# A Hymba-style block with a two-level MLP: the weight loads of the MLP move from SyncE's queue to GpSimd's

## What is computed

```python
h = rms_norm(x, attn_norm)                       # x: 1024 tokens x 1024
proj = h @ w_in                                  # 1024 x 3352
y = concat(rms_norm(nsa_mixer(...)), hgrn2_mixer(...))
x = x + y @ w_out
h = rms_norm(x, mlp_norm)
x = x + square(relu(h @ w_mlp_in)) @ w_mlp_out   # 1024 -> 4096 -> 1024
```

## Time and profile before

| | before |
|---|---|
| median of 3 runs | 1528.97 us (1526.45 to 1530.16) |
| the profiled execution's own time | 1530.4 us |
| its span, first to last instruction | 1528.6 us |
| PE busy | 1442.6 us, 94% of the span |
| DVE, ACT, POOL busy | 876.9, 629.2, 162.5 us |
| granted clock of PE, mean | 0.978 of full speed |
| loads of w_mlp_in | 32, 512 KB each, median 4.8 us from issue to landing |
| loads of w_mlp_out | 64, 256 KB each, median 5.2 us |
| loads of hidden pieces | 112, 256 KB each, median 2.7 us |
| DMAs issued by POOL | none |

### The profile page before, as it was taken

The page is one execution under the profiler, slowest core; times in us unless marked ns, Lnnn a source line. Parts: engine busy times, 40 slices in busy tenths (PEclk is TensorE's granted clock), DMA queues, the critical chain, the costliest instruction groups (busy, mean ns, idle before and its releaser), DMA issues.

```text
span 1528.6 us, 23025 instructions
## 1 busy us (share of the span) xinstructions
PE 1442.6 (94%) x7958; PEld 1233.3 (81%) x7958; DVE 876.9 (57%) x1633; ACT 629.2 (41%) x1242; POOL 162.5 (11%) x179
## 2 busy tenths in 40 slices
PE   6999999999989898998989969999999699999999
PEld 6888888878878788888978857888888588888887
DVE  2002682016666565769783485666666369668764
ACT  5014212134545444460340355755555354444441
POOL 2433333520000000000122000000000000000000
PEclk9999999999999899999999989999999899999999
DMA  4211123200000000012011013444444484843342
GB/s 163 63 48 49 48 68 91 62 7 1 2 1 0 1 0 1 0 42 111 29 42 42 29 35 127 153 146 153 153 154 148 172 303 125 275 145 97 97 118 83
DMA packets 78249, 129.25 MB, mean 85 GB/s; under 512 B 8974, under 2 KB 26827, under 8 KB 78155
## 3 DMA queue, kind: packets, MB, share of 16 engines
q1 hardware_dynamic: 77968, 128.01, 26.1%
q10 hardware_dynamic: 186, 0.08, 0.0%
HBM read 94.51 MB, written 33.55 MB: 84 GB/s over the span
## 4 chain that ended last, share of the span: by engine, by line
PE 85%; DVE 8%; issue 3%; ACT 3%; DMA 1%; DVEq 0%; SPq 0%; ACTq 0%
PE ps L516 60%; PE ps L2093 7%; PE ps L2053 4%; PE ps L2068 4%; PE ps L2116 3%; PE ps L2087 1%; PE ps L1922 1%; DVE hgrn_vg L1630 1%; PE ps L755 1%; PE ps L2058 1%; PE ps L1894 1%; PE ps L2037 1%; DVE hgrn_A L1596 0%; DVE hgrn_k L1587 0%; DVE x1T_t_low L1655 0%
## 5 line engine op out<-in xcount | busy, mean ns | idle before, releaser
L516 PE MATMUL ps<-mlp_w_high,hidden_high 128*128 128x512 f32 x448 | 174.3, 389 | 0.0
L516 PE MATMUL ps<-mlp_w_low,hidden_high 128*128 128x512 f32 x448 | 174.3, 389 | 0.0
L516 PE MATMUL ps<-mlp_w_high,hidden_low 128*128 128x512 f32 x448 | 174.3, 389 | 0.0
L516 PE MATMUL ps<-w_high,hT_high 128*128 128x512 f32 (+1 forms) x448 | 170.8, 381 | 1.6 <-DVE hT_low L1351 0.9
L516 PE MATMUL ps<-w_high,hT_low 128*128 128x512 f32 (+1 forms) x448 | 168.2, 375 | 0.0
L516 PE MATMUL ps<-w_low,hT_high 128*128 128x512 f32 (+1 forms) x448 | 168.1, 375 | 0.0
L2093 PE MATMUL ps<-nsa,probs_T 128*128 x1056 | 138.6, 276 | 0.0
L1288 ACT ACTIVATE mlp_w_high<-mlp_w_raw 128x512 fp32r<-128x512 f32 x112 | 70.8, 632 | 151.6 <-PE ps L516 143.3
L1661 DVE TENSOR_TENSOR mlp_w_low<-mlp_w_raw,mlp_w_high 128x512 fp32r<-128x512 f32 x112 | 77.1, 691 | 96.0 <-ACT mlp_w_high L1193 96.0
L2093 PEld LDWEIGHTS ps<-nsa,probs_T 128*128 128x128 f32 x1056 | 130.1, 194 | 0.0
L1741 DVE TENSOR_TENSOR mlp_w_low<-mlp_w_raw,mlp_w_high 128x512 fp32r<-128x512 f32 x112 | 77.4, 691 | 68.1 <-ACT mlp_w_high L1288 68.1
(11 more groups left out here) (232 smaller groups left out, 2936.9 us busy)
## 6 DMA issues: line engine op xcount, KB each, us to landing
hidden_raw<-hidden_pieces SPq DMA_DIRECT2D x112, 256.0 KB, 2.7
mlp_w_raw<-in_w_mlp_in_dram SPq DMA_DIRECT2D x32, 512.0 KB, 4.8
hidden_pieces<-hidden SPq DMA_DIRECT2D x64, 256.0 KB, 2.3
mlp_w_raw<-in_w_mlp_out_dram SPq DMA_DIRECT2D x64, 256.0 KB, 5.2
w_raw<-in_w_in_dram SPq DMA_DIRECT2D x56, 256.0 KB, 2.7
hidden_pieces<-hidden_s SPq DMA_DIRECT2D x48, 256.0 KB, 2.2
x_in<-in_x_dram SPq DMA_DIRECT2D x8, 512.0 KB, 6.9
w_raw<-in_w_out_dram SPq DMA_DIRECT2D x16, 256.0 KB, 2.6
```

The lines of the kernel that those rows point to most:

```text
L516: ins = nc.tensor.matmul(out_ap, a_hl[i], b_hl[j], start=first and n == 0, stop=last and n == 2, skip_group_check=onto_a_sum_already_read)
```

## The change

GpSimd issues all loads of `w_mlp_in` and `w_mlp_out`; SP keeps the stores and loads of the hidden pieces and the output. The bytes, the destinations and the semaphores that the loads raise stay the same. POOL's part comes behind its last `split_to`. The waits are these:

- `load_w1(0)` and `load_w1(1)`: as before. `load_w1(p)` for p from 2: the same count of `w1_low`, no longer behind the store of h00.
- W2 (1,1), first round: wait for product a(15), no longer between the first eight `load_h`. W2 (0,0): for b(15). W2 (0,1) and (1,0): for the end of the first product.
- second round: the same counts of `w2_lows`, no longer between `load_h`.
- SP's wait for b(15) ahead of the first `load_h` is gone; its wait for `w1_low` stays.

```diff
@@ SP @@
-            sp.wait_ge(w_used, W_OUT_AT + 8)
-            load_w1(0)
-            sp.wait_ge(xt_low, 8)
-            load_w1(1)
...
             for p in range(NPAIR):
                 sp.wait_ge(h00_ready, p + 1)
                 store(1, p, h00[p % 2][:], h00_sent[p % 2])
-                if p + 2 < NPAIR:
-                    sp.wait_ge(w1_low, IN_AT["g", p] + 1)
-                    load_w1(p + 2)
...
-            sp.wait_ge(in_done, IN_AT["b", NPAIR - 1] + 1)
             sp.wait_ge(w1_low, NPROD)
             for c in range(NCPS):
                 load_h(c)
-                load_w2((1, 1), 0, c)
             store_after_e_and_f(NPAIR - 1)
-            for c in range(NCPS):
-                load_w2((0, 0), 0, c)
             store_after_g(NPAIR - 1)
...
@@ POOL, behind its last split @@
+            def load_w1(p):
+                for j in range(2):
+                    pool.dma_start(w1_raw[:, p % 2, j, :, :], w_mlp_in[0, j * BW:(j + 1) * BW, 2 * p * P:2 * (p + 1) * P]
+                                 .rearrange("(k p) c -> p k c", p=P)).then_inc(w1_loaded[p % 2][j], 16)
+
+            pool.wait_ge(w_used, W_OUT_AT + 8)
+            load_w1(0)
+            pool.wait_ge(xt_low, 8)
+            load_w1(1)
+
+            for p in range(2, NPAIR):
+                pool.wait_ge(w1_low, IN_AT["g", p - 2] + 1)
+                load_w1(p)
...
+            pool.wait_ge(in_done, IN_AT["a", NPAIR - 1] + 1)
+            for c in range(NCPS):
+                load_w2((1, 1), 0, c)
+            pool.wait_ge(in_done, IN_AT["b", NPAIR - 1] + 1)
+            for c in range(NCPS):
+                load_w2((0, 0), 0, c)
+            pool.wait_ge(in_done, NPROD)
+            for c in range(NCPS):
+                load_w2((0, 1), 0, c)
+            for c in range(NCPS):
+                load_w2((1, 0), 0, c)
+            for first, parts in ((4, ((1, 1), (0, 0))), (5, ((0, 1),)), (6, ((1, 0),))):
+                for c in range(NCPS):
+                    pool.wait_ge(w2_lows, first * NCPS + c + 1)
+                    for q in parts:
+                        load_w2(q, 1, c)
```

More of the change, by code:

```diff
@@ L874, in _ @@
                     store_after_e_and_f(p)
[L876 to L879, removed]
             def load_h(k):
@@ L891, in _ @@
                 load_h(c)
-                load_w2((1, 1), 0, c)
             store_after_e_and_f(NPAIR - 1)
-            for c in range(NCPS):
-                load_w2((0, 0), 0, c)
             store_after_g(NPAIR - 1)
[L897 to L903, removed]
-                load_h(k)
[L905 to L917, removed]
+            for k in range(W2_RING, NPROD):
+                load_h(k)
             for g, blocks_ in ((N_OUT - 5, ((0, 0),)), (N_OUT - 2, ((1, 1), (0, 1))), (N_OUT - 1, ((1, 0),))):
@@ L978, in _, with load_w2 @@
                          m % 4, W_OUT_AT + m - m % 4 - 8 if m >= 8 else None)
+            def load_w1(p):
[9 more added lines that the diff above has]
+                load_w1(p)
+            def load_w2(q, s, c):
+                p = NCPS * s + c
+                pool.dma_start(w2_raw[q][:, c, :], w_mlp_out[0, (2 * p + q[0]) * P:(2 * p + q[0] + 1) * P, q[1] * BW:(q[1] + 1) * BW])\
+                    .then_inc(w2_loaded[q, c // 2], 16)
+            pool.wait_ge(in_done, IN_AT["a", NPAIR - 1] + 1)
[14 more added lines that the diff above has]
+                        load_w2(q, 1, c)
         @block.scalar
```

## The result

| | before | after |
|---|---|---|
| median of the runs on one chip (4 each), us | 1529.57 | 1550.28 |
| lowest to highest | 1526.45 to 1531.51 | 1547.55 to 1552.53 |
| span of the profiled execution | 1528.6 | 1545.5 |
| granted clock over the span | 0.978 | 0.977 |

The ratio is 1.0121 (95% interval 1.0099 to 1.0143): slower by 18.5 us of 1529.57 (the two medians of the table differ by 20.7), forecast +5.5. The sign was right, the size was not: it is more than three times the forecast one. The forecast started from a median of 1528.97; with the ratio that gives 1547.5 us, near the top of the stated range of 1523.5 to 1550. The table's own median, 1550.28, lies 0.3 us above that top.

A forecast was written before the change was run, and what follows sets the result against it. PE's longest waits, at the seam and early in the first product, hang on late loads; the loop's load has thin slack. Seam -5.0, early wait +0.7, loop +9.75 make +5.5 us: 1534.5 us, range 1523.5 to 1550.

The forecast's parts named there:

- W1's set-up on POOL: Each w_mlp_in load starts 0.15 to 0.8 us later when POOL issues it; taken as 0.7 us.
- PE's early wait: PE's wait ending at 915.53, early in the first product, at pair 2's weights: 12.39 us becomes 13.1.
- The slack: In the loop over pairs, the w_mlp_in load can be a mean 0.6 us later before PE waits.
- The stores beside the load: In the loop, two stores after g, now in another queue, share the load's transfer time: 0.65 us later.
- The loop: Pairs 3 to 15: load 1.35 us later, 0.6 covered, 0.75 us lost a pair, +9.75 us in all.
- the likeliest case: The forecast's own case: loop delay of 1.25 to 2.3 us, giving 1533 to 1548 us; chance 0.37.
- The seam: Between the MLP's two products, hidden pieces load without W2 beside them, PE resumes earlier: -5.0 us, bounds 4.3 and 5.7.
- The clock's cost: After the seam's wait PE runs at 1.2 GHz; taken as unchanged, a further 1.7 us were it gone.
- A: Rival: the slack holds, the loop loses nothing, the seam keeps its gain: 1521.7 to 1525.3 us; chance 0.18.
- B: Rival in between: loop delay of 0.7 to 1.25 us eats the seam's gain, 1526 to 1533 us; chance 0.30.
- C: Rival: POOL bounds the loop, by time per load row or kept from work by DVE: 1548 to 1565; chance 0.15.
- D: Rival: slow W2 loads on POOL leave no seam gain, 1539.5 us; chance within the forecast's and C's.

## Why the prediction was right or wrong

- **W1's set-up on POOL, taken +0.7 us: right.** Pair 2 gives 0.74, the kernel with both stores held a median of 0.52 over the loop. PE's early wait became 13.1, as forecast.
- **The slack, taken 0.6 us: about right.** With 0.52 us of delay PE's waits in the loop grew only from 0.6 to 1.0 us. With the change's 2.14 us they grew by 17.0 us, 1.31 a pair, which would leave 0.83 of slack.
- **The stores beside the load, taken +0.65 us: too small, and the step that failed.** I had bounded this term at 1.3 to 1.5 us "for j = 0 if all of it comes ahead, none if the load still goes first", and took half. The load was 2.14 us late in the median, 0.74 of it POOL's, which leaves 1.40; from the kernel without the stores it is 7.00 - 5.38 = 1.62. It is the upper end. The page of the skill does not say which end; the two runs with stores held do. The reason for the half was that load and stores are ready at the same time. At pair 14 the stores were issued at 1159.81 and 1160.53, 0.19 and 0.91 us behind POOL's start at 1159.62, and POOL needs 0.46 us more than SP from issue to use (pair 2): the load had no lead, and the first store's bytes went ahead of it.
- **The loop.** With 1.40 in place of 0.65 it is (0.74 + 1.40 - 0.6) x 13 = 20.0 us, for 9.75 forecast and 19.3 measured. ACT's wait for the load, which I put at about 2.9 us a pair, was 3.8 in the median. The mechanism was the forecast one: 13 gaps of PE, one a pair, for the copy of e. The delay of 2.14 us lies in the likeliest case's own span of 1.25 to 2.3 us, whose times went up to 1548, but far from the 1.35 that the sum used.
- **The seam, taken -5.0: right in kind, too large.** Measured -3.4. The second burst of W2 was in flight beside the store of a sum tile, at 7.3 us for its usual 2.3, and 1.1 us of the gain went into that. That all sixteen loads would have landed before the first hidden load was right (by 1219.2, and the first hidden load was issued at 1221.77), but I looked only at what they took from hidden loads, not at the stores under way before those. The clock's cost stayed, as taken.
- **The sum by its own terms:** -3.4 + 0.7 + 20.0 = +17.3 us, for 16.9 in the spans.
- **The rivals.** A fell: the slack held against POOL's delay, not against the stores. B fell with it: its delay of 0.7 to 1.25 us was exceeded. C gave the right size (1.7 us a pair, 1548) by the wrong mechanism: POOL's issue takes 0.75 us for one load of 512 rows, and with the stores held PE's new waits all but vanish, so neither issue time nor DVE is the cause. D fell: the seam's wait shrank.

Not settled: from DVE's sum to PE's restart the changed kernel takes 0.4 us more than the kernel with the burst held (8.72 for 8.34), and no run shows why. Why POOL's stores waited for SP's loads to end while SP's stores ran ahead of and beside POOL's is open too.

## What to carry to other kernels

In the kernel before, the order of one queue protected a load which was only just in time. Moving that load to another engine's queue put the stores which had stood behind it beside it, at about the full transfer time of each, and no engine's busy time shows it. Before moving a load, list what is issued within a microsecond of it and compare the sum of these transfer times with the slack. And where a load is late because of its place in a queue, try another place in the same queue first: here moving W2's loads alone gave 4.6 us in the same queue and 2.9 in a second one, which the measurement can't tell apart, and with the hidden loads moved too the same queue gave 12. The second queue was not tried with the hidden loads moved.

## What the runs showed of the hardware

- A 256 KB store from SP's queue, with eight W2 loads of 256 KB from POOL's queue beside it, landed in 7.3 us; with that burst held it took 2.3.
- Stores which POOL issued 0.72 and 1.45 us behind SP's load did it no harm (4.0 to 4.3 us to its use, pair 3 excepted); their queue shows no packet until the loads are nearly done. Stores which SP issued 0.19 and 0.91 us behind POOL's load cost it about 0.8 us each, the first of them by moving all its bytes ahead. Where it turns, and whether the issuing engine or the lead decides, was not measured.
- POOL took 0.75 us to issue a load of 512 rows of 1 KB and 0.54 for one of 128 rows of 2 KB, where SP took 0.47 and 0.45. The profile's page counts 61864 packets after, 78249 before, for the same bytes.
